# PEER layer: contiguous activations in the coefficient product, and coefficients as the stationary operand of the product with v

## The reference, cut to what matters

```python
ts, sel = lax.top_k(cand, PEER_TOPK)
idx = jnp.take_along_axis(cidx, sel, axis=-1)
g = jax.nn.softmax(ts, axis=-1)
act = jax.nn.gelu(jnp.einsum('chkd,cd->chk', u[idx], xt))
coef = (g * act.astype(jnp.float32)).astype(xt.dtype)
return jnp.einsum('chk,chkd->cd', coef, v[idx])
```

## Time and profile before

| what | value |
|---|---|
| runs of the kernel before | 2229.7, 2228.22, 2225.6 us |
| the profiled execution | 2226.69 us, span of its instructions 2225.4 us |
| PE busy | 97% of the span |
| DVE, ACT, POOL busy | 75%, 52%, 28% |
| granted TensorE clock | 0.995 of 2.4 GHz |
| u stage (first u matmul to last) | about 360 to 759.5 us |
| v stage | 759.6 to 1161.6 us |
| wv stage (attention, second block) | 1934.4 to 1956.2 us |

### The profile page before, as it was taken

One profiled execution on the slowest core, in us unless ns is written; L12 is line 12 of the kernel. 1 busy time (PEld: TensorE's weight loads), 2 busy tenths in 40 slices (PEclk: granted clock), 3 DMA queues, 4 the chain that ended last, 5 costly groups with the idle time before them and its releaser, 6 DMA issues.

```text
span 2225.4 us, 44628 instructions
## 1 busy us (share of the span) xinstructions
PE 2151.7 (97%) x18600; PEld 2112.7 (95%) x18600; DVE 1660.4 (75%) x2601; ACT 1161.9 (52%) x1980; POOL 626.5 (28%) x510
## 2 busy tenths in 40 slices
PE   8999999999999999999999999989999999999997
PEld 8898999999999999999999998979999999899997
DVE  7787767898998499975458656988655864787764
ACT  5776565454333434444455445746454544566443
POOL 7423254232222222223334003864002100113001
PEclk9999999999999999999999999999999999999999
DMA  5432455555444544555555554215554555544553
GB/s 168 154 129 95 162 169 168 188 178 172 155 143 161 178 146 145 168 171 181 182 181 177 185 191 131 86 33 158 190 197 145 190 190 190 180 142 146 193 194 114
DMA packets 101143, 357.35 MB, mean 161 GB/s; under 512 B 12048, under 2 KB 15440, under 8 KB 100816
## 3 DMA queue, kind: packets, MB, share of 16 engines
q1 hardware_dynamic: 100080, 352.35, 48.2%
q10 hardware_dynamic: 864, 2.16, 0.3%
HBM read 352.86 MB, written 1.05 MB: 159 GB/s over the span
## 4 chain that ended last, share of the span: by engine, by line
PE 69%; DVE 20%; POOL 4%; ACT 3%; issue 3%; DMA 1%; SPq 0%; POOLq 0%; DVEq 0%; ACTq 0%
PE PS L319 69%; DVE wlo L407 5%; DVE act L1851 3%; POOL dgl L2975 2%; DVE act L1845 2%; DVE act L1838 1%; DVE c L330 1%; DMA raw<-stream 1%; DVE ohB L1845 1%; DVE ohA L1838 1%; ACT whi L327 1%; DVE bn L2600 1%; DVE H L2649 1%; DVE w L2714 1%; DVE H L2647 1%
## 5 line engine op out<-in xcount | busy, mean ns | idle before, releaser
L407 DVE TENSOR_TENSOR wlo<-raw,whi 128x1024 fp32r<-128x1024 f32 x546 | 697.0, 1280 | 205.6 <-ACT whi L327 205.1
L327 ACT ACTIVATE whi<-raw 128x1024 fp32r<-128x1024 f32 (+1 forms) x667 | 698.8, 1050 | 199.5 <-PE PS L319 102.7
L319 PE MATMUL PS<-bn,whi 128*128 128x256 f32 x3328 | 596.1, 281 | 17.1 <-ACT bn L327 4.9
L319 PEld LDWEIGHTS PS<-bn,whi 128*128 128x128 f32 x3328 | 510.2, 188 | 23.2 <-issue 13.4
L319 PE MATMUL PS<-n,whi 128*128 128x256 f32 (+1 forms) x2784 | 515.3, 286 | 6.0 <-DVE wlo L404 3.0
L407 POOL TENSOR_TENSOR wlo<-raw,whi 128x1024 fp32r<-128x1024 f32 x119 | 319.8, 2688 | 712.6 <-ACT whi L327 712.5
L319 PE MATMUL PS<-bn,wlo 128*128 128x256 f32 x1664 | 459.6, 280 | 0.0
L319 PEld LDWEIGHTS PS<-n,whi 128*128 128x128 f32 x2784 | 434.8, 192 | 10.4 <-issue 3.5
L319 PE MATMUL PS<-n,wlo 128*128 128x256 f32 (+1 forms) x1392 | 395.0, 284 | 0.0
L319 PE MATMUL PS<-c,whi 128*128 128x256 f32 x2048 | 372.3, 284 | 0.0
L319 PEld LDWEIGHTS PS<-c,whi 128*128 128x128 f32 x2048 | 318.9, 192 | 0.0
(11 more groups left out here) (351 smaller groups left out, 3021.9 us busy)
## 6 DMA issues: line engine op xcount, KB each, us to landing
raw<-stream SPq DMA_DIRECT2D x666, 512.0 KB, 3.3
abias<-c_alibi ACTq DMA_DIRECT2D x1, 1536.0 KB, 6.5
H<-xt SPq DMA_DIRECT2D x4, 256.0 KB, 6.3
out<-H SPq DMA_DIRECT2D x3, 256.0 KB, 2.4
mask<-c_mask SPq DMA_DIRECT2D x1, 272.0 KB, 6.6
K<-Vh SPq DMA_DIRECT2D x2, 136.0 KB, 4.8
K<-Vl SPq DMA_DIRECT2D x2, 136.0 KB, 5.1
out<-H ACTq DMA_DIRECT2D x2, 128.0 KB, 1.9
```

Of the source, the lines that this page charges most:

```text
L319: return self.nc.tensor.matmul(out, l, r, start=start, stop=stop, skip_group_check=True)
L327: return self.nc.scalar.activation(out, in_, func, **kw)
L407: k.s[q].inc(me.e.tensor_tensor(lo[:, :], raw[:, :], hi[:, :].bitcast(F32), ALU.subtract))
```

## The change

Four things. (1) `multiply` walks tokens innermost: eight contiguous fp32 of a chunk, then the next chunk 1 KB further, and therefore reads its PSUM bank in steps of 64 elements; before it walked the 64 chunks innermost (steps of 1 KB in SBUF, PSUM contiguous). (2) In the v stage the coefficients (128 experts x 128 tokens) stand and the whole slab streams, 512 columns at a time: for each e four products (token block b, half f of the 1024 outputs) of three matmuls, bank 2b + f. The result now has tokens on partitions. (3) So it must be turned back: the last two e go f by f; ACT and DVE copy the four banks to `y` in SBUF, PE makes 16 transposes of 128 x 128 into banks 4 to 7, and `x_peer` adds these. (4) The banks of ffn0 lose their offset and wait for the copies and adds instead; the first product of the v stage goes to bank 0, the bank of the last u output, and `pe_pre_sums` waits for all eight adds in pre0.

```diff
@@ -66,7 +66,6 @@
 TAIL = NKEY - 16
 NBG = 72
 STEPS = NG + 2
-VBANK = [1, 0, 2, 3]
 LATE = 4
 NPE = 4
@@ -161,7 +160,7 @@
         for e in range(NKEY):
             self.col(("u", e), "uT", e)
         for e in range(NKEY):
-            self.run(("v_", e), [("v", e, m) for m in range(NC)], "each" if e == NKEY - 1 else "last")
+            self.run(("v_", e), [("v", e, m) for m in range(NC)])
     def groups(self, key, name, ms):
         self.rows((key, 0), name, ms[:4])
...
@@ -1419,7 +1418,11 @@
     p.xg_pair = [(p.xg[:, c, 0, :], p.xg[:, c, 1, :]) for c in range(NC)]
     p.n2_pair = [(p.n2[:, c, 0, :], p.n2[:, c, 1, :]) for c in range(NC)]
     p.c_pair = [(c[:, 0, :], c[:, 1, :]) for c in p.c]
-    p.out = [k.PS[:, VBANK[m // 2], NX * (m % 2):NX * (m % 2) + NX] for m in range(NC)]
+
+
+    k.low = low
+    p.y = k.place("y", [128, 2, D])
+    p.yT = [k.PS[:, 4 + m // 2, NX * (m % 2):NX * (m % 2) + NX] for m in range(NC)]
 def scored_by(i):
@@ -1542,14 +1545,43 @@
                 coefs(0, step)
         if e == 0:
             key_scores(2 * PH - 1)
-    for e in range(NKEY):
+    def products(e, wt, b, f, end=None):
+
+        c, cols = p.c[e % NCF], slice(512 * f, 512 * f + 512)
+        x = (c[:, 0, 128 * b:128 * b + 128], c[:, 1, 128 * b:128 * b + 128])
+        ins = k.mm3(PS[:, 2 * b + f, :], x, (wt[0][:, cols], wt[1][:, cols]), e == 0, e == NKEY - 1)
+        if end is not None:
+            w.end(ins, end)
+        elif e == NKEY - 1 and b == 1:
+            s["v_out"].inc(ins)
+
+    for e in range(NKEY - 2):
         P.wait_ge(s["c_lo"], e + 1)
-        for m in range(NC):
-            if e == 0 and m % 2 == 0:
-                P.wait_ge(s["gelu"], (125, 128, 126, 127)[m // 2])
-            w.mm3(p.out[m], "v", e, m, p.c_pair[e % NCF], e == 0 and m % 2 == 0, e == NKEY - 1)
-            for step in coef_tiles(1, e, m):
-                coefs(1, step)
+        wt = w.take("v", e, 0, NC)
+        for b in range(2):
+            for f in range(2):
+                if e == 0:
+                    P.wait_ge(s["gelu"], (128, 125, 126, 127)[2 * b + f])
+                products(e, wt, b, f, w.pos if b == f == 1 else None)
+                for m in range(4 * b + 2 * f, 4 * b + 2 * f + 2):
+                    for step in coef_tiles(1, e, m):
+                        coefs(1, step)
+    wts = {}
+    for e in range(NKEY - 2, NKEY):
+        P.wait_ge(s["c_lo"], e + 1)
+        wts[e] = w.take("v", e, 0, NC), w.pos
+    for f in range(2):
+        for e in range(NKEY - 2, NKEY):
+            products(e, wts[e][0], 0, f)
+            products(e, wts[e][0], 1, f, wts[e][1] if f else None)
+    P.wait_ge(s["coef"], 2 * NG)
+    for m in range(NC):
+        P.wait_ge(s["y_a"], m // 4 + 1)
+        P.wait_ge(s["y_v"], m // 4 + 1)
+        for b in range(2):
+            ins = nc.tensor.transpose(p.yT[m][:, 128 * b:128 * b + 128], p.y[:, b, 128 * m:128 * m + 128], k.ident)
+        if m % 2:
+            s["v_out"].inc(ins)
 def act_peer(k, ring):
@@ -1657,6 +1689,10 @@
             A.wait_ge(s["coef"], 2 * NG)
         ring.to(at(("v_", e), NC - 1))
         split_coef(e + NCF)
+    for f in range(2):
+        A.wait_ge(*((s["v_out"], 1) if f == 0 else (tiles, after(("v_", NKEY - 1), NC))))
+        A.wait_ge(s["cpe"], 2 * NG)
+        s["y_a"].inc(act(p.y[:, 0, 512 * f:512 * f + 512], PS[:, f, :], ACT.Copy))
     table_for(k, ACT.Sqrt)
     A.wait_ge(s["gains"], 3)
@@ -1845,10 +1881,10 @@
         s["oh"].inc(vec.tensor_tensor(out, one, rows, ALU.mult))
     def multiply(half, g):
-        v = p.halves[half][:, :].rearrange("p (i t) -> p t i", t=NX)[:, TG * g:TG * g + TG, :]
+        v = p.halves[half][:, :].rearrange("p (i t) -> p i t", t=NX)[:, :, TG * g:TG * g + TG]
         V.wait_ge(s["cpe"], NG * half + g + 1)
         V.wait_ge(s["gelu"], HK * (half + 1))
-        s["coef"].inc(vec.tensor_tensor(v, PS[:, 4 + g % 4, :].rearrange("p (t i) -> p t i", t=TG), v, ALU.mult))
+        s["coef"].inc(vec.tensor_tensor(v, PS[:, 4 + g % 4, :].rearrange("p (t i) -> p i t", t=TG), v, ALU.mult))
     def coefs(half, j):
         if j > 1:
@@ -1889,9 +1925,13 @@
         for j in coef_tiles(1, e, NC - 1):
             coefs(1, j)
     V.wait_ge(s["gains"], 3)
+    for f in range(2):
+        V.wait_ge(*((s["v_out"], 1) if f == 0 else (tiles, after(("v_", NKEY - 1), NC))))
+        V.wait_ge(s["cpe"], 2 * NG)
+        s["y_v"].inc(vec.tensor_copy(p.y[:, 1, 512 * f:512 * f + 512], PS[:, 2 + f, :]))
     for m in range(NC):
-        V.wait_ge(tiles, after(("v_", NKEY - 1), (m | 1) + 1))
-        s["x_peer"].inc(vec.tensor_tensor(k.X[m], k.X[m], p.out[m], ALU.add))
+        V.wait_ge(s["v_out"], m // 2 + 2)
+        s["x_peer"].inc(vec.tensor_tensor(k.X[m], k.X[m], p.yT[m], ALU.add))
 def pool_peer(k, ring):
@@ -2104,6 +2144,8 @@
     P, s, z = k.P, k.s, k.z
     P.wait_ge(s["stds"], STDS[pre] - 1)
+    if pre == "pre0":
+        P.wait_ge(s["x_peer"], NC)
     P.wait_ge(s["acc"], ACC_DONE[pre])
     P.wait_ge(s["sq"], SQ_BASE[pre] + NC)
     P.wait_ge(s["ysum"], YSUM["pre0" if pre == "pre0" else BEFORE[pre]])
@@ -2149,20 +2191,19 @@
 def pe_ffn(k, w, n):
     P, s, PS, z = k.P, k.s, k.PS, k.z
     base, o = GU_BASE[f"ffn{n}"], POST_BASE[FFN_POST[n]]
-    off = 4 if n == 0 else 0
     def free(i):
         if i >= 6:
             return s["gu"], base + i - 5
         if n:
             return s["pn_f"], POST_BASE[BEFORE[FFN_PRE[n]]] + NC
-        return (s["coef"], 2 * NG) if i < 2 else (s["x_peer"], 2 * VBANK.index(i - 2) + 2)
+        return [(s["y_a"], 1), (s["y_a"], 2), (s["y_v"], 1), (s["y_v"], 2), (s["x_peer"], 2), (s["x_peer"], 4)][i]
     pe_groups(k, w, ("gu", n), f"gu{n}", [m for j in range(NFF) for m in (j, NFF + j)], FFN_PRE[n], z.n,
-              lambda i: (i + off) % 6, free)
+              lambda i: i % 6, free)
     for m in range(NC):
-        P.wait_ge(*((s["gu"], base + 39 + (m - 38 - off) % 6) if m < 6 else (s["pn_f"], o + m - 5)))
+        P.wait_ge(*((s["gu"], base + 39 + (m - 38) % 6) if m < 6 else (s["pn_f"], o + m - 5)))
         for j in range(NFF):
             P.wait_ge(s["hl"], NFF * n + j + 1)
             w.mm3(PS[:, m % 6, 0:NX], f"down{n}", j, m, z.ffn[n].x[j], j == 0, j == NFF - 1)
@@ -2656,7 +2697,7 @@
 def dve_ffn(k, ring, n):
     V, s, z, f, PS, vec, tiles = k.V, k.s, k.z, k.z.ffn[n], k.PS, k.nc.vector, k.s["tiles"]
-    key, o, off = ("gu", n), NFF * n, 4 if n == 0 else 0
+    key, o = ("gu", n), NFF * n
     for r in range(NC):
         ring.to(at((key, 0, r), 3))
     dve_pre_std(k, FFN_PRE[n])
@@ -2668,7 +2709,7 @@
     def job(i):
         j, up = divmod(i, 2)
         V.wait_ge(tiles, after((key, 0, NC - 1), i + 1) if i < 4 else after((key, i), NC))
-        ps = PS[:, (i + off) % 6, 0:NX]
+        ps = PS[:, i % 6, 0:NX]
         if not up:
             if j >= 3:
                 V.wait_ge(s["sil"], o + j - 2)
```

More of the change, by code:

```diff
@@ L265 @@
     "u scan gate_f att hr hr_hi hr_lo rn mix mix_hi mix_lo x_att key_hi key_lo gains q2_hi q2_lo kscore "
-    "sc n2_g n2_r n2_hi n2_lo gelu tr_r r_act gp oh cpe coef c_hi c_lo x_peer ysum f_sq pairs gu sil h hh_hi "
+    "sc n2_g n2_r n2_hi n2_lo gelu tr_r r_act gp oh cpe coef c_hi c_lo x_peer v_out y_a y_v ysum f_sq pairs gu sil h hh_hi "
     "hl rs restored x_new pn_f dgh dgl diag w_act cen cen_q ln_var ln_d silu ln_hi ln_lo colsum "
```

## The result

The changed kernel takes 2198.7 us (median of 4 runs, 2193.5 to 2200.5), the kernel before 2229.0 beside it (4 runs, 2225.6 to 2231.0): ratio 0.986 [0.984, 0.988], so 1.4% less and clear of the spread of the runs, with 2199 forecast. Its profiled execution takes 2197.6 us with a span of 2196.3, 29.1 less than the span before. The sum had said 29.9.

The account below looks back on a forecast made before the run. PE was taken to bound the kernel, except where DVE was late in stretches with coefficient steps. Terms summed to -29.9 us: 2226.7 to 2196.8, plus 1.5 for the runs' median, stated as 2199; own range 2191 to 2207, wider 2190 to 2220.

Parts of the forecast that it names:

- u stretch: u stage, e = 64 to 111, with coefficient steps: 7.5 of PE's 9.4 us of waits were to go.
- v stage, 61.8 e with steps: v stretch, from the v stage's start to 971 us: 196 us instead of 211.5, 15.5 gained (10 to 20.6).
- v stage behind the steps: Rest of the v stage after 971 us, 66.2 e: PE sets the pace, 10.6 us gained.
- wait for the last gelu: Start of the v stage: PE's first product waits for the last u output's gelu, 0.7 us lost.
- last product to ffn0: End of the v stage: ACT's queue of rounding, copies, table and `bn` delays ffn0, 3 us lost (2 to 5).
- The multiply: DVE's multiply in the coefficient steps: 1331 ns falls to 0.68 us, PSUM's step free (bounds 676 and 1986 ns).
- Rivals 1 to 3: PSUM's step costs: multiply about 1.0 us (2207, chance 0.12); 1331 ns (2219, 0.14); 1986 ns (2261, 0.08).
- 512 columns: v stage matmuls at the wv stage's 0.2268 us: 0.16 us less per e, 20.3 us if PE sets the pace throughout.
- Rival 4: Behind 971 us slab loads become the bound and the 10.6 us gain vanishes: 2209 us, chance 0.04.
- the group: One group of coefficient matmuls on PE: adds 0.71 us, 22.7 us for 32 groups.
- 5 above PE's need: v stretch: PE needs 190.9 us, DVE 187; both nearly full never interlock well, so 196 was taken.
- The cover: Shorter multiply hides less of POOL's hold-ups of DVE: 8 cases at 0.6 us, 5 us back in each stretch.

## Why the prediction was right, point by point

| term | predicted | measured |
|---|---|---|
| u stretch | -7.5 | -6.9 |
| v stage, 61.8 e with steps | -15.5 | -14.4 |
| v stage behind the steps | -10.6 | -10.6 |
| wait for the last gelu | +0.7 | +0.6 |
| last product to ffn0 | +3.0 | +2.7 |
| sum | -29.9 | -28.6 |

- **The multiply.** 0.68 us were taken between bounds of 0.676 and 1.986, because the excess of 655 ns was put down to SBUF alone. It measures 0.684. The argument held further than needed: one stepped stream of SBUF costs 394 ns by itself, and a step in PSUM none that can be seen. Rivals 1 to 3 fall with this row, and each would have shown: at about 1.07 us, 1.33 or above.
The Trainium skill's rule that any non-contiguous pattern in PSUM slows matmuls significantly (PSUM — Partial Sum Buffer, Specifications) doesn't carry over to DVE's reads: every element here lies on a line of its own and the read costs 684 ns against 676.
- **512 columns.** The wv stage's pace of 0.2268 us carried over: behind the steps PE is busy for 169.2 of 169.2 us and the stretch is 10.6 us shorter. Rival 4 falls: the slabs came at 194 GB/s, above the 183 of the earlier trace rows, with no hole in PE.
- **The u stretch.** The mechanism is the one forecast: DVE's load fell below PE's, to 148.3 us, and the waits for its tables went. All of them went, not 7.5 of 9.4. But the 9.4 were too many: a group costs PE 0.78 us, not 0.71, so PE needs 163.8 and not 161.5, and the waits were 7.2. The term that was mis-sized is the group: it was read only up to the start of the next product, which is late itself. Two errors met, waits counted too high and a rest of 1.9 that isn't there.
- **The v stretch.** 196 forecast, 197.0 measured, for a reason that is only in part the one given. The step of the prediction that failed is "5 above PE's need" of 190.9, put down to two nearly full engines that don't interlock. PE's need is 61.8 x 2.72 + 32 x 0.83 = 194.7, and the kernel with POOL freed takes 195.1. So about 4 of the 6.1 us above 190.9 are the price of switching between small and large matmuls, and about 2 are DVE's lateness. The forecast was saved by a margin for the wrong cause. The interlocking itself is real, 4.8 us over the larger load, where the two loads are 1.5 us apart (old multiply with POOL freed, 193.6 and 195.1). The prediction took them to be 3.9 apart (187 and 190.9); with PE's need put right they are 9.8 apart, and it costs 1.9.
- **The cover.** A shorter multiply was to give 5 us back in each stretch, since POOL's low parts would hold up other operations more. It gave back 2.0 in the u stretch (21 less 19.0) and 3.8 in the v stretch (21 less 17.2). The sign was right and the size too large. DVE's load of 187 in the v stretch came out at 185.3. That the 148 of the u stretch came out at 148.3 is partly luck: it was worked out from a window of 167 us, and the whole stretch had 167.3 us of DVE before, not 163.5.
- **The start.** PE's first product waits 0.56 us for the gelu, as the trace of before had it.
- **The tail.** The chain of ACT named in the prediction is the one that the rows show: rounding to 0.2 us before the end of the last product, two copies, table, `bn`. The copies took 0.53 us each and not 0.65, so ffn0 begins 2.8 us behind the end of the last product where 3.2 were forecast. That PE waits for ACT's queue is shown by the experiment that moves the table and the first copy ahead. The transposes take about 0.12 us each and not 0.095, and are covered all the same. The 0.3 us from F to ffn0 in the kernel before are 0.2 with the matmul that has no record.
- **The range.** Its own terms add up to 2190 and 2208 us, not 2191 and 2207; nothing hangs on it.

What the waits in the kernel before were, in the end, is two causes of one size. The slow multiply filled DVE, and POOL held DVE up at the moments when PE was waiting. Either removed alone brings both stretches to PE's floor or within 1.2 us of it (163.9 and 393.6 or 394.8 us); the second then brings nothing there. In the turned product, where PE needs less, the freed POOL alone leaves 4.8 us and the new multiply alone 1.9. The prediction named POOL's hold-ups only as something that the change would lose a little to. It didn't see that they were a lever as large as the change's own multiply.

What stays open: why the switch costs PE more at 512 columns (0.12 us) than at 256 (0.07).

## What to carry to other kernels

Where an element-wise operation of DVE in fp32 takes one operand from PSUM and walks SBUF in steps of 1 KB, give the step to PSUM and keep SBUF in runs of at least 16 bytes, which cost nothing here. Halving the time of such an operation is worth only what the engine behind it still waits for, so work out that engine's floor from a stretch without waits, its switches between kinds of matmul included. When DVE is late, look also for operations of DVE far above their median: here taking 39 low parts off POOL, though DVE then had more to do, gave as much as a multiply of half the length.

## What the hardware showed that was not expected

- DVE reads PSUM with a step of 256 bytes at full pace: 684 ns for 128 x 512 in fp32, against 676 contiguous.
- DVE with a step of 1 KB in SBUF, 512 elements: 1070 ns with one stepped stream, read or write alike, 1331 with both. Runs of 2 values 710, of 4 values 683.
- POOL's low parts hold up DVE by more than they would cost it: 20 of them moved to DVE lower its busy time from 202.6 to 194.6 us.
- Behind a group of small bf16 matmuls the large fp32r products cost 0.07 us more at 256 columns and 0.12 at 512, once for each switch; at 512 columns it is 0.12 whether the group has 24 or 12.
- 16 transposes of 128 x 128 in fp32 in a row take 1.94 us, 0.12 each, where six of them took 0.57, 0.095 each.
- PE and DVE, each waiting for the other's results, take 4.8 us over the larger load in a stretch of 200 us when their loads are 1.5 us apart (no low parts on POOL), and 1.9 us when they are 9.8 apart (with POOL's low parts).
